# Weight pieces of 32 KB a partition in four places, w_down by column halves, and top-k on two partitions an expert

## What is computed

```
def expert_choice_moe(h, w_router, w_gate, w_up, w_down):
    B, L, D = h.shape
    cap = EC_CAPACITY * L // N_EXPERTS_2
    aff = jax.nn.softmax(h.astype(F32) @ w_router.astype(F32), axis=-1)
    gate, idx = lax.top_k(aff.transpose(0, 2, 1), cap)
    xs = jax.vmap(lambda hb, ib: hb[ib])(h, idx)
    a = jnp.einsum('becd,edf->becf', xs, w_gate)
    b = jnp.einsum('becd,edf->becf', xs, w_up)
    y = jnp.einsum('becf,efd->becd', jax.nn.silu(a) * b, w_down)
    y = y * gate.astype(y.dtype)[..., None]
    return jax.vmap(lambda yb, ib: jnp.zeros((L, D), yb.dtype).at[ib.reshape(-1)].add(
        yb.reshape(-1, D)))(y, idx)
```

## Time and profile before

| | us |
|---|---|
| median of three runs | 2909.63 |
| the profiled execution | 2904.43 |
| its span in the trace | 2902.6 |
| expert layer, from its first weight load to the end | 1913.9 to 2902.6 |
| TensorE busy in the whole span | 2656.8 (92%) |
| weights moved in the expert layer | 402.7 MB |

### The profile page before, as it was taken

The page is one execution under the profiler, slowest core; times in us unless marked ns, Lnnn a source line. Parts: engine busy times, 40 slices in busy tenths (PEclk is TensorE's granted clock), DMA queues, the critical chain, the costliest instruction groups (busy, mean ns, idle before and its releaser), DMA issues. The chain is left out here.

```text
span 2902.6 us, 34245 instructions
## 1 busy us (share of the span) xinstructions
PE 2656.8 (92%) x13197; PEld 1868.4 (64%) x13197; DVE 1403.2 (48%) x2355; ACT 853.9 (29%) x1431; POOL 696.5 (24%) x427
## 2 busy tenths in 40 slices
PE   7988889999999989999999799769998989989896
PEld 4846779999999978888888676543332333333332
DVE  4456449997778838888888435450000000010001
ACT  4244323336777723333333323410000000000001
POOL 0231016767888842222221020000000000000000
PEclk9989999999999989999999899879999999999999
DMA  7164215558999999999997221169999999999996
GB/s 291 40 233 147 87 58 172 170 183 285 358 383 384 373 359 354 356 366 355 358 357 282 79 88 71 58 259 381 428 428 427 428 428 427 428 428 428 428 427 260
DMA packets 211622, 860.27 MB, mean 296 GB/s; under 512 B 21047, under 2 KB 90679, under 8 KB 183592
## 3 DMA queue, kind: packets, MB, share of 16 engines
q1 hardware_dynamic: 156200, 699.18, 61.8%
q0 software_dynamic: 36864, 134.23, 12.0%
q10 hardware_dynamic: 18432, 25.17, 2.4%
HBM read 805.02 MB, written 53.49 MB: 296 GB/s over the span
## 5 line engine op out<-in xcount | busy, mean ns | idle before, releaser
L962 PE MATMUL val_banks<-val_v,val_coef_split 128*128 128x512 f32 x2268 | 517.1, 391 | 9.5 <-DVE val_coef_split L95 9.5
L962 PEld LDWEIGHTS val_banks<-val_v,val_coef_split 128*128 128x128 f32 x2268 | 427.7, 189 | 98.8 <-DVE val_v L95 9.8
L1223 PE MATMUL moe_up_ps<-all_raw_first,moe_xs_t 128*64 128x512 f32 x1632 | 436.8, 614 | 41.6 <-DMA all_raw_first<-in_up_tiles 31.8
L725 PE MATMUL dots_dot_ps<-both_acts,dots_u_split 128*128 128x384 f32 x2064 | 376.5, 339 | 16.7 <-POOL dots_u_split L95 16.7
L725 PEld LDWEIGHTS dots_dot_ps<-both_acts,dots_u_split 128*128 128x128 f32 x2064 | 361.3, 190 | 19.3 <-issue 10.0
L1223 PEld LDWEIGHTS moe_up_ps<-all_raw_first,moe_xs_t 128*64 128x64 f32 x1632 | 141.1, 141 | 287.1 <-issue 286.1
L95 POOL TENSOR_TENSOR dots_u_split<-dots_u_raw,dots_u_split 128x1024 fp32r<-128x1024 f32 x86 | 226.7, 2637 | 242.8 <-ACT dots_u_split L90 241.8
L1358 DVE TENSOR_TENSOR all_x<-moe_y_ps,all_x 128x512 f32<-128x512 f32 x64 | 44.0, 691 | 445.5 <-PE moe_y_ps L1191 445.4
L90 ACT CAST val_v<-both_shared 128x2048 fp32r<-128x2048 f32 x64 | 122.1, 1907 | 346.2 <-PE val_banks L962 346.2
L1429 POOL DMA_INDIRECT val_v_rows<-in_peer_v,one_expert x128 | 133.0, 1039 | 377.1 <-DVE val_banks L867 360.3
L1240 PE MATMUL moe_y_ps<-all_raw_first,moe_hid_t 128*64 128x512 f32 x768 | 198.4, 608 | 4.9 <-issue 3.7
(11 more groups left out here) (391 smaller groups left out, 3321.8 us busy)
## 6 DMA issues: line engine op xcount, KB each, us to landing
all_raw_first<-in_gate_tiles SPq DMA_DIRECT2D x51, 2048.0 KB, 30.7
all_raw_first<-in_up_tiles SPq DMA_DIRECT2D x51, 2048.0 KB, 31.0
all_raw_first<-in_w_down SPq DMA_DIRECT2D x48, 2048.0 KB, 33.1
both_shared<-in_peer_v SPq DMA_DIRECT2D x64, 1024.0 KB
dots_u_raw<-in_u_tiles SPq DMA_DIRECT2D x86, 512.0 KB
moe_raw_more<-in_w_down SPq DMA_DIRECT2D x16, 2048.0 KB, 32.1
moe_raw_more<-in_gate_tiles SPq DMA_DIRECT2D x13, 2048.0 KB, 29.7
moe_raw_more<-in_up_tiles SPq DMA_DIRECT2D x13, 2048.0 KB, 33.3
```

What stands on the lines that cost most here:

```text
L725: last = self.nc.tensor.matmul(self.banks[:, q % 2, 0:DENSE], self.split[q % 3][:, u_part, k], self.h_t[:, h_part, k, T - DENSE:T], start= ...
L962: last = nc.tensor.matmul(banks[:, 2 * (t + 1) + half, :], coef_split[:, b, c_part, a, t * P:(t + 1) * P], v[:, b, v_part, a, half * BANK: ...
L1223: last = nc.tensor.matmul(up_ps[of(e), b, :], xs_t[:, k, of(e)], w[e][:, b * BANK:(b + 1) * BANK], start=(k == 0), stop=(k == KD - 1))
```

## The change

The pieces grow to PER = 4 units, 4 MiB in runs of 32 KB a partition. The ring has four places (three early, one more in `moe_phase`) in place of nine, 128 KB a partition in place of 144. Gate and up tiles are laid out on the host as four input tiles a piece, and w_down as two column halves of 512: a down piece now holds all sixteen hidden tiles for one half of the output columns. So u = 16 to 19 compute the first 512 columns of y and u = 20 to 23 the second. The last piece of each expert is loaded in five parts (three units, then two half units), and the last four units wait for these parts.

For the last pair, the first column half is spread right after u = 20 (into `up_ps` banks), added, squared and multiplied by the gain, and ScalarE scales it, while VectorE scales the second half; SP waits for both halves of a tile.

The choice puts the two halves of 256 tokens of each expert on two partitions (32 in all), finds the 64 best of each half in eight rounds as before, moves the second half's list to the first 16 partitions by one matmul, and merges: of the sorted lists, the larger of the i-th of one and the i-th from the end of the other.

```diff
 class ExpertPieces:
 
-    FIRST, MORE = 7, 2
+    FIRST, MORE = 3, 1
     UNITS = 24
-    PER = 2
+    PER = 4
     SIZE = PER * FF
 
     def __init__(self, nc, s, A):
@@ -1038,21 +1038,35 @@
         self.slots = [s.sb(f"raw_first{i}", [P, self.SIZE]) for i in range(self.FIRST)]
         self.ring = self.FIRST + self.MORE
         self.loaded = [s.sem(f"piece_loaded{i}") for i in range(self.ring)]
+        self.total = 2 * self.UNITS * NPAIR // self.PER
+        self.ends = ((0, FF), (FF, 2 * FF), (2 * FF, 3 * FF), (3 * FF, 3 * FF + FF // 2), (3 * FF + FF // 2, 4 * FF))
+        self.end_loaded = [s.sem(f"end_loaded{i}") for i in range(len(self.ends))]
...
+    def source(self, n):
 
         groups = self.UNITS // self.PER
         i, u, e = n // (2 * groups), n // 2 % groups, n % 2
-        if u < 8:
-            m, k = ("gate", "up")[u // 4], u % 4
-            src = self.A[f"{m}_tiles"][2 * i + e, k]
-        else:
-            src = self.A["w_down_2"][0, 2 * i + e].rearrange("(p j) n -> p j n", p=P)[
-                :, 4 * (u - 8):4 * (u - 8) + 4, :].rearrange("p j n -> p (j n)")
-        sp.dma_start(self.slots[n % self.ring][:], src).then_inc(self.loaded[n % self.ring], 16)
+        if u < 4:
+            m, k = ("gate", "up")[u // 2], u % 2
+            return self.A[f"{m}_tiles"][2 * i + e, k]
+        return self.A["down_tiles"][2 * i + e, u - 4]
+
+    def load(self, sp, n):
+        sp.dma_start(self.slots[n % self.ring][:], self.source(n)).then_inc(self.loaded[n % self.ring], 16)
+
+    def load_end(self, sp, used):
+
+        for (first, end), sem in zip(self.ends, self.end_loaded):
+            for n in (self.total - 2, self.total - 1):
+                if first == 0:
+                    self.wait_free(sp, n, used)
+                sp.dma_start(self.slots[n % self.ring][:, first:end], self.source(n)[:, first:end]).then_inc(sem, 16)
+
+    def wait_end(self, eng, part):
+        eng.wait_ge(self.end_loaded[part], 32)
...
-                for n in range(pieces.ring, 2 * UNITS * NPAIR // pieces.PER):
+                for n in range(pieces.ring, pieces.total - 2):
                     pieces.wait_free(sp, n, used)
                     pieces.load(sp, n)
+                pieces.load_end(sp, used)
                 sp.wait_ge(xs_turned, 2 * NPAIR)
                 sp.dma_start(g_rows, rows(A["final_g_2"], P)).then_inc(g_loaded, 16)
                 for t in range(NT):
                     sp.wait_ge(row_ready, t + 1)
+                    sp.wait_ge(first_ready, t + 1)
...
-                        last = nc.tensor.transpose(aff_ps[:, t * P:(t + 1) * P], aff[:, t, :], ident[:])
+                    for a in range(2):
+                        last = nc.tensor.transpose(left_ps[:, a * P:(a + 1) * P],
+                                                   aff[:, a].rearrange("p h e -> p (h e)"), ident[:])
                     last.then_inc(aff_turned, 1)
+                    pe.wait_ge(half_ready, 1)
+                    nc.tensor.matmul(late_ps, ident[0:2 * NE, NE:2 * NE], best, start=True,
+                                     stop=True).then_inc(half_moved, 1)
                     pe.wait_ge(best_ready, 1)
                     for e in range(2):
                         of_half = ident[0:NE, e:NE:2]
-                        nc.tensor.matmul(list_ps[of(e), 0:NPAIR], idx_f[:], of_half, start=True, stop=True)
-                        last = nc.tensor.matmul(list_ps[of(e), NPAIR:2 * NPAIR], val[:], of_half, start=True, stop=True)
+                        nc.tensor.matmul(list_ps[of(e), 0:NPAIR], idx_f, of_half, start=True, stop=True)
+                        last = nc.tensor.matmul(list_ps[of(e), NPAIR:2 * NPAIR], val, of_half, start=True, stop=True)
...
+                def spread_end(half):
+
+                    pe.wait_ge(spread_ready, NPAIR)
+                    pe.wait_ge(y_taken, LAST + half + 1)
+                    for t in range(NT):
+                        if half == 1:
+                            pe.wait_ge(added, 8 * LAST + t + 1)
+                        nc.tensor.matmul(up_ps[:, t, :], spread[:, t * P:(t + 1) * P],
+                                         y[:, half * BANK:(half + 1) * BANK], start=True,
+                                         stop=True).then_inc(spread_done, 1)
...
+                        if NPAIR * UNITS - 4 <= q < NPAIR * UNITS - 1:
+                            pieces.wait_end(pe, q - NPAIR * UNITS + 4)
+                        elif u % pieces.PER == 0 and q < NPAIR * UNITS - 4:
                             for e in range(2):
                                 pieces.wait(pe, q, e)
...
-                            if u % 2 == 0:
-                                pe.wait_ge(hid_t_ready, i * 4 + (u - 16) // 2 + 1)
-                            for k in range(2):
-                                j = (u - 16) * 2 + k
-                                for half in range(2):
-                                    for e in range(2):
-                                        last = nc.tensor.matmul(
-                                            y_ps[of(e), half, :], hid_t[:, j, of(e)],
-                                            w[e][:, k * D + half * BANK:k * D + (half + 1) * BANK],
-                                            start=(j == 0), stop=(j == KF - 1))
...
+                        elif u == 20:
+                            spread_end(0)
+                spread_end(1)
...
+                def take_half(half):
+                    act.wait_ge(used, LAST * UNITS + 16 + 4 * (half + 1))
+                    if half == 0:
+                        act.wait_ge(spread_done, 8 * LAST)
+                    nc.scalar.copy(y[:, half * BANK:(half + 1) * BANK], y_ps[:, half, :]).then_inc(y_taken, 1)
+
+                def square(t, half):
+                    act.wait_ge(added, 8 * LAST + NT * half + t + 1)
+                    if half == 1:
+                        act.wait_ge(squared, t + 1)
+                    nc.scalar.activation(silu[:, t, :], x[:, t, half * BANK:(half + 1) * BANK], ACT.Square,
+                                         accum_out=mean[:, half, t:t + 1]).then_inc(squared, 1)
+
+                def root_of(t):
+                    act.wait_ge(mean_ready, NT + t + 1)
+                    nc.scalar.activation(root[:, t:t + 1], mean[:, 1, t:t + 1], ACT.Sqrt).then_inc(root_ready, 1)
+
+                def scale_first(t):
+                    act.wait_ge(rstd_ready, t + 1)
+                    nc.scalar.activation(x[:, t, 0:BANK], x[:, t, 0:BANK], ACT.Copy,
+                                         scale=out_rstd[:, t:t + 1]).then_inc(first_ready, 1)
+
+                take_half(0)
                 for t in range(NT):
-                    act.wait_ge(added, 8 * (NPAIR - 1) + 2 * t + 2)
-                    if t >= 2:
-                        act.wait_ge(squared, t - 1)
-                    nc.scalar.activation(silu[:, 2 * (t % 2):2 * (t % 2) + 2, :],
-                                         x[:, t, :].rearrange("p (a n) -> p a n", a=2), ACT.Square,
-                                         accum_out=mean[:, t:t + 1]).then_inc(squared, 1)
-                    act.wait_ge(mean_ready, t + 1)
-                    nc.scalar.activation(root[:, t:t + 1], mean[:, t:t + 1], ACT.Sqrt).then_inc(root_ready, 1)
+                    square(t, 0)
+                take_half(1)
+                square(0, 1)
+                for t in range(NT):
+                    root_of(t)
+                    if t + 1 < NT:
+                        square(t + 1, 1)
+                    scale_first(t)
...
+                    left, rest = left_ps, aff_t[0:2 * NE, 0:T // 2]
                     for r in range(CAP // 8):
                         eight = slice(8 * r, 8 * r + 8)
-                        step(nc.vector.max(val[:, eight], left))
-                        step(nc.vector.max_index(idx[:, eight], val[:, eight], left))
+                        step(nc.vector.max(best[:, 0, eight], left))
+                        step(nc.vector.max_index(idx[:, eight], best[:, 0, eight], left))
                         if r < CAP // 8 - 1:
-                            step(nc.vector.match_replace(aff_t[0:NE, :], val[:, eight], left, -1.0))
-                        left = aff_t[0:NE, :]
-                    nc.vector.tensor_copy(idx_f[:], idx[:]).then_inc(best_ready, 1)
+                            step(nc.vector.match_replace(rest, best[:, 0, eight], left, -1.0))
+                        left = rest
+                    nc.vector.tensor_copy(best[:, 1, :], idx).then_inc(half_ready, 1)
+                    dve.wait_ge(half_ready, 1)
+                    dve.wait_ge(half_moved, 1)
+                    early, early_idx = best[0:NE, 0, :], best[0:NE, 1, :]
+                    late, late_idx = late_ps[:, 0, ::-1], late_ps[:, 1, ::-1]
+                    nc.vector.tensor_tensor(val, early, late, ALU.max)
+                    nc.vector.tensor_tensor(later, early, late, ALU.is_lt)
```

(41 more changed lines are left out.)

57 lines of the change are left out of this document (33 added, 24 removed).

## The result

| | before | changed |
|---|---|---|
| median of four runs each, us | 2908.09 | 2963.91 |
| ratio, with its 95% interval | 1 | 1.0202 (1.0182 to 1.0222) |
| the profiled execution, us | 2904.43 | 2962.46 |
| its span, us | 2902.6 | 2960.6 |
| TensorE's mean granted clock | 0.96 | 0.952 |

The account below looks back on a forecast made before the run. The DMA engines, at 428 GB/s, were taken to bound the expert layer. Terms 6.4 + 4.9 - 4.5 + 40 + 2.0 made +49 on the profiled 2904.4, so 2953; forecast median 2955 us, range 2922 to 2976.

Parts of the forecast that it names:

- Choice: Token choice ahead of u0: searches over 256 columns in place of 512, net 4.6 us less (+1.5 to -5).
- Restart: First refill of the queue: waits for four units and a selection in place of two units, 6.4 us later.
- Places: Ring: four places hold 16 MiB instead of 18, one 2 MiB piece more after the first refill, +4.9 us.
- Longer runs: DMA transfers: 32 KB runs lower packet cost, 0.5% of 903 us, -4.5 us (0 to -17).
- rival 2: Queue from 1974 on: run length limits the engines; decides from 1.3% gain, 2899 up to 2904; 6 in 100.
- Two groups: Each expert pair: work plus refill delay exceeds transfer, queue runs dry; 5.75 us a pair, +40 for seven (14 to 68).
- The latency: Refills in each pair: delay beyond transfer of 2.6 us (2.0 to 3.3), from the first 2 MiB refill.
- Tail: Behind the last landing: eight down units +7.1, early column half -5.1, together +2.0 us (0 to +4).
- The median: Whole kernel: median of three runs stands 5.2 us above the profiled run; 2955 forecast for the median.
- against 1: Rival: the queue never runs dry, latency hidden, the +40 goes; 2911.5, up to 2917 for the median; 7 in 100.
- against 3: Rival: TensorE's clock holds through waits of 5 us; each pair loses 3.2, 22 in all, 2933; 22 in 100.
- Rival 4: TensorE's clock falls at each wait and for longer: 68 in place of 40, tail +4, 2983; 10 in 100.

Follow-up runs that it names:

- full queue: Changed kernel with most expert products left out, all weights still loaded, so TensorE is never late: 2891.59 us, ratio 0.9962.
- four extra products: Changed kernel with four unread products ahead of the wait at u16 and half of the selection's products left out: 2950.50 us, ratio 1.0152.

## Why the prediction was right, and where its sum was off

The direction and the cause held, and the size nearly: 55.8 us against 46 (2955 less the median of 2909). In the layer the forecast was +49 and the trace shows +62.0, so the layer's sum was 13 short, and it is chance that only part of this shows in the time. Step by step:

- **Choice, -4.6.** The two rows of the changed kernel that answer to the earlier trace rows:

```profile
1928.94 0.42 DVE L1402 MAX8 moe_y<-moe_y_ps 32x8 f32<-32x256 f32 x1 [0.49 <-PE moe_y_ps L1173]
```

```profile
1951.92 7.09 PE L1262 MATMUL moe_up_ps<-all_raw_first,moe_xs_t 128*64 128x512 f32 x32 [0.68 <-ACT moe_xs_t L1313]
```

  MAX8 took 0.42, as the additions' slope had said. From the router's load, u0 began 43.9 us on, before 48.0: -4.0; alone the choice brought 5.5 by the medians and 3.8 in the layer.
- **Restart, +6.4.** Measured +6.75. The engines stood from about 1953 to 1970, 17 us, where 16 were foretold:

```profile
1956.00:1969.00 13.00, 13.00 (x77) 6.58 (x74) 0.00 (x0) 1.87 (x2) 0.00 (x0) 1.00 0.01 1
```

- **Places, +4.9.** Nine places against eight, both with 16 KB: 6.5 us by the medians and 3.3 in the layer, on both sides of 4.9.
- **Longer runs, -4.5.** Measured 0.8%, so -7, where 0.5% stood; rival 2's 1.3% was not reached. The full queue's 431 GB/s stays under the 435 that the Trainium skill (DMA: Bandwidth & Descriptors, Where 436 GB/s comes from) names as the ceiling of the sixteen ports; the trace agrees with that figure.
- **Two groups, +40.** This is the term that was mis-sized. The middle stretch gives 53.2 - 4.9 + 7 = **+55**. The two main holes stand where they were foretold, but together larger: around the refills after u19 and u23 4.0 and 2.1 us, where 2.4 (0.7 and the clock's 1.7) and 2.0 stood. Around the refill after u7 it is 1.2, where 1.35 stood for u4 to u7; around the one after u15 it is 1.0, where nothing stood. Two steps failed:
  1. *The latency.* I took 2.6 from one refill of 2 MiB. The loads of the fourth place, which end a group of 8 MiB, took 21.4 to 23.1 us in the seven pairs, with a median of 22.7, against 19.5 for the group's bytes at 431 GB/s: 2.0 to 3.6, median 3.2. In the pair whose chain is shown it was only 2.0. The first load of a gate group, 4 MiB, took 12.1 to 13.9 against 9.7: 2.4 to 4.2. My bounds of 2.0 and 3.3 had no second row behind them, and the one row is a piece of another size. With 3.2 in place of 2.6 in both of its terms a pair would have lost 6.95 (an estimate from these numbers).

```profile
moe_raw_more<-in_gate_tiles SPq DMA_DIRECT2D x7, 4096.0 KB, 22.7
```

  2. *One ring only.* I reckoned each pair as a sum of excesses over transfer for one order of groups. With two groups each delay feeds the next refill. I had said that u8 to u15 lose nothing; a wait of 7.2 us ahead of u12 (forecast 3.5 to 5.5) and its slow clock, behind which the hole of 1.0 lies, were in no term.

```profile
2261.53 1.08 PE L1262 MATMUL moe_up_ps<-all_raw_first,moe_xs_t 128*64 128x512 f32 x1 [7.16 <-DMA moe_raw_more<-in_up_tiles]
```

  By bytes, 283.24 MB where a full queue moved 301.72 are 42.9 us lost in 700, or 7.65 a pair, where 5.75 stood; times seven 53.5.
- **Tail, +2.0.** Measured +2.0. From u16's landing at 2908.46 to the last y at 2944.2 are 35.7 (forecast 35.3), 16 behind the last landing (15.7), and 16.4 from there to the end of the span (16.8). Before, 21.9: the early column half brought the 5 us.
- **The median.** The prediction says that the median stands 5.2 above the profiled run, but 2953 and 5.2 make 2958, not 2955; the 3 us less have no reason in it. Here the two profiled runs lie 3.7 and 1.5 under theirs, and the stages ahead were 4.0 shorter in one of them. These chances hide part of the 13 us by which the layer's sum was short.
- **One reading.** Of the "last fourteen" slices of the earlier trace rows eleven stand at 427 or 428 GB/s; the others are 259 and 381 around the start of the layer and 260 at the end. Nothing in the sum hangs on it.
- **The rivals.** The queue runs dry (against 1). Runs of 32 KB gain 0.8%, not 1.3 (against 2). The clock fell behind the waits ahead of u12 and u16 (against 3). Rival 4's price for the groups, 68, was too high: it priced the slow clock behind u16's wait at 3.4, and in the seven pairs the first unit there and its turns took 1.3 to 2.8 longer than at full clock. The Trainium skill (Trainium Kernel Development and Optimization, Best Practices) asks for double-buffering; here two groups of either length moved 405 and 364 GB/s (ratios 1.0202 and 1.0570), and three or more 427 to 430 (0.9991, 1.0023, 0.9995 and 0.9964; the 1.0023 has the smallest first fill of them, 12 MiB). So the measurement goes against it where work and turnaround exceed the transfer.

## What to carry to other kernels

A ring of buffers must be counted in groups that are waited for and freed together: two are enough only if the work on one group, with everything that stands in the same program order and the refill's latency, is shorter than its transfer. Enlarging pieces in the same memory trades groups for run length; here the runs gave 7 us and the groups took 55. Where two resources feed each other, a cost that is taken away can come back as a wait in another ring of like length: look at which refills the chain runs through before and after. And when an edit adds work of its own, change nothing else in the next run: here four extra products in place of five took away the proof.

## What the runs showed of the hardware

- Runs of 24 KB and 32 KB a partition moved 0.5% and 0.8% more than 16 KB in 700 us of full queue (300.94 and 301.72 against 299.39 MB).
- A group of 8 MiB in 32 KB runs, asked for when the queue had run dry or nearly so, landed 2.0 to 3.6 us later than its bytes at the full rate (seven pairs, median 3.2); two groups of 4 MiB in 16 KB runs 3.1 and 2.4 (12.87 and 12.23 against 9.8); one refill of 2 MiB 2.6.
- Keeping TensorE busy with products that nobody reads kept the granted clock at full (1.00; 1.14 and 3.65 us in place of 1.94 and 5.01), and taking 1.9 us of work from each selection lowered it elsewhere (0.50; 6.54 us for 3.65 behind a wait of 5.54).
- MAX8 over 256 columns on 32 partitions took 0.42 us, over 512 on 16 partitions 0.69.
